# Two transformer blocks on one core: part-wise waits in the first experts' loop over further blocks, row stores without landing waits, and one exponential per head in the scan chunks

## The chip, the cores and the metric

The kernel runs on one core of a Trainium2 chip. The metric is device time in microseconds (us) of one execution. The kernel before took 2706.3 us (median of 3 runs, 2701.29 to 2710.79). The engines are TensorE (PE; its weight loads are listed as PEld), VectorE (DVE), ScalarE (ACT), GpSimd (POOL) and SyncE (SP, which issues most DMAs). A name with a q (SPq, PEq) is that engine's sequencer.

## What is computed

Two blocks in a row on 512 tokens of width 1024. The first mixes latent attention and a retention, then 32 routed experts (4 per token). The second mixes a bidirectional Mamba-2 scan with grouped attention, then 16 routed experts. Three places matter here: the modulation rows, one expert block, and the part of the scan inside a chunk of 128 tokens.

```
mod = (silu(c) @ w_ada + b_ada).reshape(B, 6, 1, D)        # same for c_ctx, and for the second block's w_mod

def expert_block(args):                                     # 32 rows of one expert at a time in the kernel
    tok, g, e = args
    u = (h_pad[tok] @ w1[e] + b1[e])
    glu = minimum(u[:, 0::2], 7); lin = clip(u[:, 1::2], -7, 7)
    act = glu * sigmoid(1.702 * glu) * (lin + 1.0)
    y = act @ w2[e] + b2[e]

# scan, one direction (the other runs on flipped inputs with its own dt and A), per chunk:
xdt = xs * dt[..., None]
a_cs = cumsum(dt * A)
decay = where(lower, exp(where(lower, a_cs[q] - a_cs[s], 0)), 0)
cb = einsum('bcqgn,bcsgn->bcqsg', Cc, Bc)
y_diag = einsum('bcqsgr,bcsgrp->bcqgrp', cb[..., None] * decay, xdt)
```

## The kernel before, in words

The program is a sequence of stages. `stage` opens a block with one instruction stream per engine; the next stage begins when all five streams have come to their end, so a wait at the end of SP's stream holds every engine. Inside a stage the streams are ordered by semaphores alone.

**Modulations.** `Modulations` spreads six groups of work g over stages of the first mixer. A group is four weight pieces of 2 MB (`load`, `load_after`), their products on PE (`product`), a bias product, a copy of the sum from PSUM to `kept[g % 2]` on ACT (`keep`), a turn into columns on PE (`turn`) and a copy of these on ACT (`keep_columns`). Some chunks are also stored as rows in DRAM (`store_rows`): groups 1 and 2 store two rows of 512 numbers, groups 4 and 5 four, groups 0 and 3 none. Group 1 is stored at the end of the stage "ret_prep" (just before the retention's loop), group 2 at the end of "ret_out" (just before the stage "latents"), groups 4 and 5 at the end of the head norms.

**First experts.** `first_expert_blocks` has 80 blocks of 32 rows laid out ahead, 31 turns of six weight chunks each (UC = 4 of `w_mlp1`, WC = 2 of `w_mlp2`, 2 MB a chunk, a ring of 11 slots). Then comes a loop over further blocks, whose number the router decides (`over_count`, never less than one). One pass of the loop loads six chunks and a bias of 8 KB, gathers and turns the rows, runs the first product on the four chunks of `w_mlp1`, the activation on DVE and ACT, and the second product on the two chunks of `w_mlp2`. The trace has 192 chunk loads, 31 x 6 + 6, so the loop runs once. Before the change the seven loads of a pass share one semaphore, and both PE and DVE wait for all of it:

```
pe.wait_ge(s.over_landed, i * (16 * LOADS) + 16 * LOADS)      # LOADS = per + 1 = 7
```

**Chunks of the scan.** `within_chunks` (stage "within") walks over eight pairs m: four token tiles t by two groups g, eight heads (r) in a pair. The exponents of both directions are formed against rows in `weight_slots`, which `load_scan` brings from DRAM, 2 MB for a tile. Per pair, DVE lowers the forward exponents below zero (`lower`, eight instructions), ACT cuts the backward ones (eight Relu), ACT takes two exponentials, DVE multiplies both by the masked product `cb`, and PE multiplies the two matrices of each head with `xdt`, which POOL made from `xs` and `dt`. `keep` masks `cb` twice and `add` adds PE's sum to the output, both on DVE.

## Time and profile before

| | us |
|---|---|
| median of 3 runs | 2706.3 (2701.29 to 2710.79) |
| the profiled execution | 2707.46 |
| its span, first to last instruction | 2705.7 |
| PE busy | 2176.6 (80%) |
| DVE busy | 1049.1 (39%) |
| ACT busy | 728.7 (27%) |
| POOL busy | 256.1 (9%) |

The trace is of one execution. Its times are counted from the span's start. Busy shares are means over stages that have different limits; three short stretches matter here: about 190 to 203 and 267 to 298 us (row stores), 1596 to 1652 us (the loop over further blocks) and 2229 to 2302 us (the scan chunks). A line of the timeline may merge several instructions of one kind; its second column is then from the start of the first to the end of the last. "Idle before" is the time in which the engine had nothing to run, and the name behind the arrow is what ended it.

### The profile page before, as it was taken

The page shows a single profiled execution, that of the slowest core. Times are in us where ns is not written, and L with a number is a line of the kernel's source. Part 1 is how long each engine was busy: PE and PEld are TensorE (multiplying, and loading weights), DVE is VectorE, ACT ScalarE, POOL GpSimd, SP SyncE. Part 2 cuts the span into 40 slices and gives each one's busy share as a digit, 9 for nine tenths or more (in the row PEclk, how much of TensorE's full clock was granted, in tenths as well). Part 3 has the DMA queues.
Part 4 walks back from the last instruction along what each step waited for, and adds up shares of the span by engine and source line. Part 5 has one row for each costly group of instructions (what it writes and reads, how often), then busy time and mean ns, then how long its engine had stood idle before and what let it go on. Part 6 is the DMA issues. An engine that isn't in the chain of part 4 may idle for free. (4 is left out here: it accounts for less than half of the span.)

```text
span 2705.7 us, 43890 instructions
## 1 busy us (share of the span) xinstructions
PE 2176.6 (80%) x18172; PEld 1252.9 (46%) x18172; DVE 1049.1 (39%) x1937; ACT 728.7 (27%) x1816; POOL 256.1 (9%) x223
## 2 busy tenths in 40 slices
PE   4979679839998998988989874799899768393795
PEld 2965247633333333333333331588766528382342
DVE  2235465442222222222222223454266567625343
ACT  3213456221110110110110100352266644412222
POOL 0001000000000000000000002000199131000001
PEclk8988879959999999998998986899999885696897
DMA  5345620138999999999999994322000011201995
GB/s 216 110 187 198 264 103 1 70 131 338 421 421 420 417 421 423 420 421 421 421 421 421 421 405 165 121 93 78 1 1 1 1 63 63 109 32 49 391 419 214
DMA packets 146299, 628.56 MB, mean 232 GB/s; under 512 B 33396, under 2 KB 64372, under 8 KB 92344
## 3 DMA queue, kind: packets, MB, share of 16 engines
q1 hardware_dynamic: 117832, 580.28, 52.9%
q0 software_dynamic: 8064, 29.36, 2.8%
q10 hardware_dynamic: 20208, 16.15, 1.8%
q8 instruction: 143, 2.34, 0.4%
q14 instruction: 52, 0.43, 0.0%
HBM read 592.37 MB, written 33.38 MB: 231 GB/s over the span
## 5 line engine op out<-in xcount | busy, mean ns | idle before, releaser
L2121 PE MATMUL psum<-w,x 128*32 128x512 f32 x5184 | 621.4, 627 | 127.5 <-DMA w<-in_w_mlp 105.5
L2121 PEld LDWEIGHTS psum<-w,x 128*32 128x32 f32 x5184 | 164.1, 113 | 526.0 <-issue 354.0
L2277 DVE TENSOR_TENSOR u<-psum,x 128x512 f32<-128x512 f32 x81 | 56.0, 691 | 707.2 <-PE psum L2121 707.2
L731 PE MATMUL psum<-high 128*128 128x512 f32 (+3 forms) x832 | 293.5, 353 | 38.7 <-DVE low L753 37.5
L2130 PE MATMUL psum<-w,act_turned 128*32 128x256 f32 x5184 | 297.3, 382 | 3.8 <-DVE act_turned L2286 3.5
L731 PE MATMUL psum<-low,high 128*128 128x512 f32 (+3 forms) x832 | 293.1, 352 | 0.0
L731 PE MATMUL psum<-high,low 128*128 128x512 f32 (+3 forms) x832 | 292.5, 352 | 0.0
L2130 PEld LDWEIGHTS psum<-w,act_turned 128*32 128x32 f32 x5184 | 168.4, 111 | 160.5 <-issue 62.4
L753 DVE TENSOR_TENSOR low<-weight_slots,high 128x1024 fp32r<-128x1024 f32 (+3 forms) x84 | 89.2, 1066 | 264.8 <-ACT high L747 264.2
L731 PEld LDWEIGHTS psum<-high 128*128 128x128 f32 x832 | 159.7, 192 | 61.1 <-ACT high L747 39.5
L731 PEld LDWEIGHTS psum<-low,high 128*128 128x128 f32 x832 | 160.0, 192 | 21.0
L2218 ACT ACTIVATE sig<-glu 128x256 f32<-128x256 f32 x81 | 34.5, 426 | 500.5 <-DVE glu L2278 500.3
L731 PEld LDWEIGHTS psum<-high,low 128*128 128x128 f32 x832 | 159.4, 192 | 21.3
L747 ACT CAST high<-weight_slots 128x1024 fp32r<-128x1024 f32 (+3 forms) x84 | 77.0, 921 | 295.2 <-PE psum L731 287.4
L2209 ACT ACTIVATE x<-psum,cols,scale1f 128x128 f32<-128x128 f32 x160 | 58.2, 470 | 205.4 <-PE psum L2121 170.5
L1203 ACT ACTIVATE weight_slots<-psum,shifts 128x768 f32<-128x768 f32 x96 | 86.7, 903 | 66.5 <-DVE shifts L1255 66.3
L2092 POOL DMA_INDIRECT x<-token_rows,slot_token x20 | 19.0, 948 | 903.3 <-PE psum L2112 879.6
L344 PE MATMUL psum<-weight_slots,mix 128*32 128x512 f32 x384 | 58.9, 755 | 56.2 <-DMA weight_slots<-in_w_ada 32.0
L1254 DVE TENSOR_REDUCE peaks<-psum 128x1 f32<-128x768 f32 x96 | 91.5, 953 | 26.9 <-PE psum L1123 26.4
L2226 ACT COPY x<-psum 128x256 f32<-128x256 f32 x80 | 29.8, 373 | 242.2 <-DMA slot_rows<-x 152.9
L2432 PE MATMUL psum<-gu,turned 128*32 128x512 f32 x656 | 82.6, 623 | 13.1 <-ACT turned L2565 5.4
L1134 PE MATMUL psum<-ident,weight_slots 128*128 128x128 f32 x576 | 85.3, 278 | 3.7 <-ACT weight_slots L1203 3.2
(497 smaller groups left out, 2846.8 us busy)
## 6 DMA issues: line engine op xcount, KB each, us to landing
w<-in_w_mlp SPq DMA_DIRECT2D x192, 2048.0 KB, 28.8
weight_slots<-in_w_ada SPq DMA_DIRECT2D x12, 2048.0 KB, 10.8
weight_slots<-in_w_mod SPq DMA_DIRECT2D x12, 2048.0 KB, 10.9
weight_slots<-in_w_in SPq DMA_DIRECT2D x9, 2048.0 KB, 8.8
gu<-in_w_gate SPq DMA_DIRECT2D x16, 1024.0 KB, 28.5
gu<-in_w_up SPq DMA_DIRECT2D x16, 1024.0 KB, 30.5
down<-in_w_down SPq DMA_DIRECT2D x16, 1024.0 KB, 31.9
weight_slots<-in_w_out SPq DMA_DIRECT2D x6, 2048.0 KB, 11.3
```

The lines of the kernel that those rows point to most:

```text
L344: mm = pe.matmul(out[c * 32:(c + 1) * 32], self.c[:, which, kp * self.KP + i, :], rows[:, i, c * BANK:(c + 1) * BANK], start=kp == 0 and i ...
L731: mm = pe.matmul(psum[:, p.group % 8, 0:p.width], *p.operands(x, weights[:, n % 2], u * QK_ + kc, kc), start=p.first and u == 0 and kc == ...
L747: act.copy(w.high[:, n % 2, :, 0:chunks[j].source.shape[2]], piece(j, u)).then_inc(s.high_made, 1)
L753: dve.tensor_tensor(w.low[at], piece(j, u), w.high[at].bitcast(F32), ALU.subtract).then_inc(s.low_made, 1)
L1134: mm = pe.transpose(turned_ps[j % 2][:, t * P:(t + 1) * P], probs[head % 2][:, t, j * P:(j + 1) * P], k.ident[:])
L1203: act.activation(probs[c][:, t], rows_ps[t % 2], ACT.Exp, scale=scale, bias=b.shifts[:, c, t:t + 1], accum_out=b.sums[:, c, t:t + 1]).then ...
L1254: step(dve.tensor_reduce(b.peaks[:, c, t:t + 1], rows_ps[t % 2], AX, ALU.max))
L2121: mm = pe.matmul(psum[g * RB:(g + 1) * RB, bank, :], b.turned[:, kc, q * RB:(q + 1) * RB], w[:, i, g * BANK:(g + 1) * BANK], start=kc == 0 ...
L2130: mm = pe.matmul(psum[g * RB:(g + 1) * RB, 2 + parity, 0:YW], b.act_turned[:, parity, kc, :], w[:, i, g * YW:(g + 1) * YW], start=kc == 0, ...
L2209: ins = act.activation(b.turned[:, m, :], psum[:, 4 + m // 4, (m % 4) * P:(m % 4 + 1) * P], ACT.Identity, scale=k.scale1f[:, m:m + 1], bia ...
L2277: step.reach(dve.tensor_tensor(b.u[:], psum[:, bank, :], b.bias[:], ALU.add), s.biased, at + 1)
L2432: mm = pe.matmul(psum[g * RB:(g + 1) * RB, bank, :].rearrange("p (a n) -> p a n", a=2), b.turned[:, half, kc, q * RB:(q + 1) * RB], b.gu[: ...
```

## The change

There are three edits. `store_rows` no longer waits for its rows to land, except for the last group; the next store waits for the earlier ones, and the `keep` that writes a buffer again waits for the stores that read it. In the loop over further blocks the bias is requested ahead of the six chunks and has a semaphore of its own; the chunks share three semaphores by twos, and PE waits for the first pair, the second pair, and ahead of the second product the third. In the scan chunks the smaller of the forward and backward exponents is taken, one exponential is made of it, the factors `dt` of both directions go into a weight matrix with `cb`, and PE multiplies one matrix per head with `xs` itself; POOL has no work there any more.

```diff
--- before.py
+++ after.py
@@ -288,6 +288,7 @@
...
         self.landed, self.rows_stored = {}, 0
+        self.stored_by = {}
     def chunks_kept_as_rows(self, g):
...
@@ -329,10 +330,14 @@
...
         sync.wait_ge(self.k.mod_kept, g + 1)
+        if self.rows_stored:
+            sync.wait_ge(self.k.mod_stored, self.rows_stored)
         for c, lo in self.chunks_kept_as_rows(g):
...
             self.rows_stored += 16
-        sync.wait_ge(self.k.mod_stored, self.rows_stored)
+        self.stored_by[g] = self.rows_stored
+        if g == len(self.work) - 1:
+            sync.wait_ge(self.k.mod_stored, self.rows_stored)
     def product(self, pe, j):
@@ -365,6 +370,9 @@
...
             act.wait_ge(self.k.mod_turned, g - 1)
+            if self.stored_by.get(g - 2):
+                act.wait_ge(self.k.mod_stored, self.stored_by[g - 2])
         act.copy(self.kept[g % 2], self.core.psum[:, self.SUM_BANK[g], :]).then_inc(self.k.mod_kept, 1)
...
@@ -2004,7 +2012,6 @@
...
     RING = 11
-    LOADS = per + 1
     BC = BANK // RB
...
@@ -2028,9 +2035,12 @@
...
                   "clipped", "squashed", "act_ready", "y_kept", "x_turned", "x_kept", "y_stored", "vector_step",
-                  pool_dma=("gathered", "slots_free", "over_landed", "ids_made", "taken")) as (block, s):
+                  pool_dma=("gathered", "slots_free", "over_bias_landed", "over0_landed", "over1_landed", "over2_landed",
+                            "ids_made", "taken")) as (block, s):
         landed = [[s.landed0_0, s.landed0_1, s.landed0_2, s.landed0_3, s.landed0_4, s.landed0_5],
                   [s.landed1_0, s.landed1_1, s.landed1_2, s.landed1_3, s.landed1_4, s.landed1_5]]
+        over_landed = [s.over0_landed, s.over1_landed, s.over2_landed]
         def wait_landed(engine, turn, c):
@@ -2069,17 +2079,16 @@
...
                 e = sync.value_load(r.blocks[0:1, ds(i, 1)], min_val=0, max_val=E1 - 1)
+                sync.wait_ge(s.bias_spread, i + turns)
+                sync.sem_inc(s.taken, 1)
+                sync.dma_start(b.bias_in_over[:], bias_of(e)).then_inc(s.over_bias_landed, 16)
                 for c in range(per):
...
                     sync.dma_start(b.w[:, (turns * per + c) % RING].rearrange("p (k n) -> p k n", k=src.shape[1]), src)\
-                        .then_inc(s.over_landed, 16)
-                sync.wait_ge(s.bias_spread, i + turns)
-                sync.sem_inc(s.taken, 1)
-                sync.dma_start(b.bias_in_over[:], bias_of(e)).then_inc(s.over_landed, 16)
+                        .then_inc(over_landed[c // 2], 16)
         @block.gpsimd
...
@@ -2185,15 +2194,19 @@
...
                 pe.wait_ge(s.x_kept, i + (tiles + 1))
-                pe.wait_ge(s.over_landed, i * (16 * LOADS) + 16 * LOADS)
                 pe.wait_ge(s.biased, i + n)
...
                 for c in range(UC):
+                    if c % 2 == 0:
+                        pe.wait_ge(over_landed[c // 2], i * 32 + 32)
+                        pe.sem_inc(s.taken, 1)
                     first_chunk(turns, c, 0, 0).then_inc(s.slots_free, 1)
...
                 pe.wait_ge(s.y_kept, i + n)
+                pe.sem_inc(s.taken, 1)
+                pe.wait_ge(s.over2_landed, i * 32 + 32)
                 pe.sem_inc(s.taken, 1)
...
@@ -2302,7 +2315,7 @@
...
                 step.restart()
-                dve.wait_ge(s.over_landed, i * (16 * LOADS) + 16 * LOADS)
+                dve.wait_ge(s.over_bias_landed, i * 16 + 16)
                 dve.sem_inc(s.taken, 1)
...
@@ -3179,30 +3192,27 @@
...
+    n = len(pairs)
...
+    with buffers(core, decay=[P, HELD, SR * P], back=[P, 2, SR * P], weight=[P, 2, SR * P], cb=[P, 2, 2, P]) as b, \
+            stage(core, "within", "cb_summed", "cb_kept", "backward", "tinted", "lowered", "weighted", "exped", "joined",
+                  "summed", "added") as (block, s):
+        def row(t, d, g, r):
+            c = d * SH + g * SR + r
+            return core.ring.slots[:, t % 2].rearrange("p k n -> p (k n)")[:, c * P:(c + 1) * P]
+        def column(v, t, d, g, r):
+            c = d * SH + g * SR + r
+            return v[:, t, c:c + 1]
         @block.sync
         def _(sync):
...
+                sync.wait_ge(s.backward, SG * (t - 1))
...
         @block.tensor
         def _(pe):
@@ -3213,43 +3223,69 @@
...
+                pe.wait_ge(s.joined, m + 1)
...
+                    mm = pe.matmul(psum[:, 4 + m % 2, r * SP_:(r + 1) * SP_], b.decay[:, m % HELD, r * P:(r + 1) * P],
+                                   xs[:, t, (g * SR + r) * SP_:(g * SR + r + 1) * SP_], start=True, stop=True)
...
         @block.scalar
         def _(act):
...
+            def backward(m):
+                t, g = pairs[m]
...
+                if m >= 2:
+                    act.wait_ge(s.lowered, m - 1)
...
+                    ins = act.activation(b.back[:, m % 2, r * P:(r + 1) * P], row(t, 1, g, r), ACT.Identity,
+                                         bias=column(w.fallen, t, 1, g, r))
+                ins.then_inc(s.backward, 1)
+            def tint(m):
+                t, g = pairs[m]
+                act.wait_ge(s.cb_kept, 2 * m + 2)
+                if m >= 2:
+                    act.wait_ge(s.joined, m - 1)
+                for r in range(SR):
+                    ins = act.activation(b.weight[:, m % 2, r * P:(r + 1) * P], b.cb[:, m % 2, 1], ACT.Copy,
+                                         scale=column(w.dt, t, 1, g, r))
+                ins.then_inc(s.tinted, 1)
+            def exponential(m):
...
+                act.activation(b.decay[:, m % HELD], b.decay[:, m % HELD], ACT.Exp).then_inc(s.exped, 1)
+            backward(0)
+            tint(0)
+            exponential(0)
+            backward(1)
+            tint(1)
+            for m in range(n):
+                if m + 1 < n:
+                    exponential(m + 1)
+                if m + 2 < n:
+                    backward(m + 2)
+                    tint(m + 2)
         @block.vector
         def _(dve):
+            def keep(m):
+                if m % 4 == 0:
+                    dve.wait_ge(s.cb_summed, m // 4 + 1)
+                if m >= 2:
+                    dve.wait_ge(s.tinted, m - 1)
+                    dve.wait_ge(s.weighted, m - 1)
+                for d in range(2):
+                    dve.tensor_tensor(b.cb[:, m % 2, d], psum[:, 6 + m // 4, (m % 4) * P:(m % 4 + 1) * P],
+                                      k.after[:] if d else k.upto[:], ALU.mult).then_inc(s.cb_kept, 1)
             def lower(m):
...
@@ -3257,23 +3293,24 @@
...
+                dve.wait_ge(s.backward, m + 1)
...
+                    at = slice(r * P, (r + 1) * P)
+                    ins = dve.scalar_tensor_tensor(out=b.decay[:, m % HELD, at], in0=row(t, 0, g, r),
+                                                   scalar=column(w.fallen, t, 0, g, r), in1=b.back[:, m % 2, at],
+                                                   op0=ALU.add, op1=ALU.min)
...
+            def weigh(m):
+                t, g = pairs[m]
+                dve.wait_ge(s.tinted, m + 1)
+                dve.wait_ge(s.cb_kept, 2 * m + 2)
+                for r in range(SR):
+                    at = slice(r * P, (r + 1) * P)
+                    ins = dve.scalar_tensor_tensor(out=b.weight[:, m % 2, at], in0=b.cb[:, m % 2, 0],
+                                                   scalar=column(w.dt, t, 0, g, r), in1=b.weight[:, m % 2, at],
+                                                   op0=ALU.mult, op1=ALU.add)
+                ins.then_inc(s.weighted, 1)
             def add(m):
...
@@ -3281,24 +3318,24 @@
...
+            keep(0)
+            keep(1)
...
+            weigh(0)
+            for m in range(n):
+                if m + 1 < n:
...
+                dve.wait_ge(s.exped, m + 1)
+                dve.wait_ge(s.weighted, m + 1)
+                dve.tensor_tensor(b.decay[:, m % HELD], b.decay[:, m % HELD], b.weight[:, m % 2], ALU.mult)\
+                    .then_inc(s.joined, 1)
+                if m + 1 < n:
+                    weigh(m + 1)
...
+                if m + 2 < n:
+                    keep(m + 2)
+            add(n - 1)
...
```

SP's issues in one pass of the loop over further blocks, before (`w` are the chunks, `x<-in_b_mlp` is the bias; each ISA row is a semaphore step):

```order
L2077 DMA w<-in_w_mlp 128x4096
L2074 REGISTER_ALU
L2077 ISA
L2077 DMA w<-in_w_mlp 128x4096
L2080 REGISTER_ALU
L2082 ISA
L2082 DMA x<-in_b_mlp 128x16
```

And now, from the same pass:

```order
L2084 ISA
L2084 DMA x<-in_b_mlp 128x16
L2087 ISA
L2090 ISA
L2090 DMA w<-in_w_mlp 128x2x2048
L2087 REGISTER_ALU
L2090 ISA
L2090 DMA w<-in_w_mlp 128x2x2048
```

The bias moved from behind the sixth chunk to ahead of the first.

ACT in the scan chunks, the first pairs, before (L3242 is the Relu on the backward exponents, L3246 and L3248 are the exponentials):

```order
L3242 ACTIVATE decay<-weight_slots,running 128x128 x8
L3246 ACTIVATE decay<-decay 128x1024
L3248 ACTIVATE decay<-decay 128x1024
L3242 ACTIVATE decay<-weight_slots,running 128x128 x8
L3246 ACTIVATE decay<-decay 128x1024
```

And now (L3245 is `backward`, L3256 `tint`, L3262 the one exponential):

```order
L3245 ACTIVATE back<-weight_slots,fallen 128x128 x8
L3256 ACTIVATE weight<-cb,dt 128x128 x8
L3262 ACTIVATE decay<-decay 128x1024
L3245 ACTIVATE back<-weight_slots,fallen 128x128 x8
L3256 ACTIVATE weight<-cb,dt 128x128 x8
L3262 ACTIVATE decay<-decay 128x1024
```

One exponential of a pair went, eight narrow activations came.

DVE in the scan chunks, one pair in the middle, before (L3262 `lower`, L3295 the multiplications by `cb`, L3274 `keep`, L3282 `add`):

```order
L3282 TENSOR_TENSOR raw<-raw,psum 128x512
L3262 SCALAR_TENSOR_TENSOR decay<-weight_slots,fallen,zero 128x128 x8
L3295 SCALAR_TENSOR_TENSOR decay<-decay,cb 128x1024 x2
L3274 TENSOR_TENSOR cb<-psum,upto 128x128
L3274 TENSOR_TENSOR cb<-psum,after 128x128
```

And now (L3299 `lower`, L3330 the one multiplication, L3310 `weigh`, L3319 `add`, L3286 `keep`):

```order
L3299 SCALAR_TENSOR_TENSOR decay<-weight_slots,fallen,back 128x128 x8
L3330 TENSOR_TENSOR decay<-decay,weight 128x1024
L3310 SCALAR_TENSOR_TENSOR weight<-cb,dt,weight 128x128 x8
L3319 TENSOR_TENSOR raw<-raw,psum 128x512
L3286 TENSOR_TENSOR cb<-psum,upto 128x128
L3286 TENSOR_TENSOR cb<-psum,after 128x128
```

One wide multiplication of a pair went, eight narrow instructions of `weigh` came, and `keep` moved to the pair's end, two pairs ahead.

## Rows read from the trace of the kernel before

**Rows 1.** Timeline, end of "ret_prep": start us, length us, engine, line, what [idle before].

```profile
192.66 0.56 SPq L333 DMA_DIRECT2D rows<-mix  x2
...
194.60 0.19 ACT L374 COPY cols<-psum 128x32 f32<-128x32 f32 x1 [1.96 <-PE psum L358]
202.59 1.28 ACT L1399 ACT_TABLE_LOAD   x1 [7.80 <-PEq L168]
```

**Rows 2.** Timeline, from the end of the retention to the end of "latents".

```profile
267.89 1.91 ACT L1533 ACTIVATE squares<-mix 128x2048 f32<-128x2048 f32 x1 [0.44 <-ACT mix L1411]
...
274.45 0.38 SPq L308 DMA_DIRECT2D weight_slots<-in_w_mod  x1
...
275.14 0.56 SPq L333 DMA_DIRECT2D rows<-mix  x2
...
279.61 2.29 DVE L1551 TENSOR_TENSOR mix<-mix,gate 128x2048 f32<-128x2048 f32 x1
...
287.88 4.97 PE L344 MATMUL psum<-weight_slots,mix 128*32 128x512 f32 x32 [6.97 <-PEq L168]
...
295.64 0.19 ACT L374 COPY cols<-psum 128x32 f32<-128x32 f32 x1 [1.15 <-PE psum L358]
296.24 0.61 DVE L857 TENSOR_SCALAR pc<-pc,rates 128x128 f32<-128x128 f32 x2
```

**Rows 3.** DMA view, the load issued at 274.45: size, us from issue to landing.

```profile
weight_slots<-in_w_mod SPq DMA_DIRECT2D x1, 2048.0 KB, 13.1
```

**Rows 4.** Timeline, the loop over further blocks.

```profile
1602.56 0.34 SPq L2077 DMA_DIRECT2D w<-in_w_mlp  x1
1603.23 0.33 SPq L2082 DMA_DIRECT2D x<-in_b_mlp  x1
...
1615.68 2.26 ACT L2249 ACTIVATE x<-psum,cols,scale1f 128x32 f32 x8 [3.31 <-issue]
...
1631.65 8.94 PE L2121 MATMUL psum<-w,x 128*32 128x512 f32 x64 [18.69 <-DMA x<-in_b_mlp]
...
1643.29 0.63 DVE L2286 STREAM_TRANSPOSE act_turned<-act 128x256 f32<-128x256 f32 x1 [0.24 <-DVE act L2283]
...
1644.07 3.66 PE L2130 MATMUL psum<-w,act_turned 128*32 128x256 f32 x64 [3.47 <-DVE act_turned L2286]
```

**Rows 5.** DMA view, the two issues at 1602.56 and 1603.23.

```profile
w<-in_w_mlp SPq DMA_DIRECT2D x1, 2048.0 KB, 23.3
...
x<-in_b_mlp SPq DMA_DIRECT2D x1, 8.0 KB, 28.2
```

**Rows 6.** Stage view of "within": us, busy PE, PEld, DVE, ACT, POOL, PEclk, DMA, GB/s.

```profile
2229.00:2301.00 72.00, 59.11 (x272) 58.33 (x272) 55.40 (x105) 34.96 (x80) 15.23 (x8) 0.52 0.15 59
```

**Rows 7.** Groups by line, same stage: count | busy us, mean ns | idle before.

```profile
L3223 PE MATMUL psum<-xdt,decay 128*128 128x64 f32 x256 | 55.4, 422 | 12.1 <-DVE decay L3295 12.1
...
L3282 DVE TENSOR_TENSOR raw<-raw,psum 128x512 f32<-128x512 f32 x8 | 5.5, 683 | 16.2 <-PE psum L3223 16.2
```

**Rows 8.** Timeline, the scan chunks.

```profile
2229.26 7.62 POOL L3202 TENSOR_TENSOR xdt<-xs,dt 128x1024 f32<-128x1024 f32 x4 [21.62 <-POOLq L168]
...
2229.54 8.54 DVE L3262 SCALAR_TENSOR_TENSOR decay<-weight_slots,fallen,zero 128x128 f32<-128x128 f32 x8
...
2238.40 2.17 DVE L3262 SCALAR_TENSOR_TENSOR decay<-weight_slots,fallen,zero 128x128 f32<-128x128 f32 x8
...
2240.50 2.35 DVE L3295 SCALAR_TENSOR_TENSOR decay<-decay,cb 128x1024 f32<-128x1024 f32 x2
...
2243.16 2.17 DVE L3262 SCALAR_TENSOR_TENSOR decay<-weight_slots,fallen,zero 128x128 f32<-128x128 f32 x8
...
2244.25 2.43 ACT L3242 ACTIVATE decay<-weight_slots,running 128x128 f32<-128x128 f32 x8
...
2246.59 1.04 ACT L3246 ACTIVATE decay<-decay 128x1024 f32<-128x1024 f32 x1
...
2301.59 1.28 ACT L3319 ACT_TABLE_LOAD   x1 [16.74 <-PEq L168]
```

61 lines of the change are left out of this document (removed).

## The prediction

> **What bounds the kernel now.** I read the slices first: PE is busy 80% of the span, but the edits do not touch the long matmul stretches. So I read the timeline of each stage that the diff names, looking for what ends the last wait there.
>
> At the end of "ret_prep" SP issues two small row stores at 192.66 and the last engine, ACT, ends at 194.79; nothing runs until ACT starts at 202.59 [rows 1]. The reader is to see a stage held open by the landing of 4 KB. "ret_out" repeats it: stores at 275.14, DVE ends at 281.90, the next stage opens at about 287.87 [rows 2]. The stores sit behind 2 MB weight pieces; the one issued at 274.45 needs 13.1 us and lands at 287.55 [rows 3].
>
> In the loop over further blocks PE starts at 1631.65, ended by the bias, though the rows it multiplies were ready at 1615.68 + 2.26 = 1617.94 [rows 4]. The sixth chunk, issued at 1602.56, lands 23.3 us later at 1625.9, the bias, issued last at 1603.23, at 1631.4 [rows 5]. In the scan chunks PE is busy 59.11 of 72 us with DVE close behind at 55.40, at a granted clock of 0.52, so 1.2 GHz nearly throughout [rows 6]. PE's 256 matmul records there take 55.4 us, 0.216 each [rows 7]. DVE loses time to something besides: the first eight `lower` take 8.54 us while POOL runs four multiplications, the second eight 2.17 without POOL [rows 8].
>
> **Part A, the row stores.** A stage opens 0.44 us after the last engine's end (ACT at 267.89) [rows 2]. "ret_prep" without SP's wait ends with ACT at 194.79, so the retention starts at 195.23 instead of 202.59: −7.4. What is late next there? The retention's own modulation products read pieces requested well before, and its first work needs no DMA, so I charge nothing; if it waited for the piece still in flight, which is what held the stage, the loss would be all 7.4.
>
> "ret_out" ends at 281.90, so "latents" opens 5.5 us earlier, at 282.34. But PE's second half of the products there needs the piece that lands at 287.55 [rows 3]. The 32 records took 4.97 us, so half of them 2.5 by the mean, 0.6 less or 0.8 more by the clock they get (estimates around that mean). PE's products end at 289.4 to 290.8 instead of 292.85. From there to the column copy's end is 295.83 − 292.85 = 3.0 us, some 1.7 more if its two PE groups run at the low clock: 292.4 to 295.5. DVE's end moves to 296.85 − 5.5 = 291.3. The stage ended at 296.85; it now ends by PE's chain, between 1.4 and 4.5 earlier; I take the middle, −3.0. In the head norms the final wait stays and the edit moves nothing: 0. The added waits on ACT are for stores long landed: 0. A = −10.4, bounds −3 and −12.
>
> The Trainium skill (DMA: Bandwidth & Descriptors, section on the anatomy of one DMA) gives a small DMA a fixed cost of about 2.0 us. An estimate by that page would let the stores land at about 195.2, 0.4 us behind ACT's end, and part A would be worth 0.4 us at its first place. The trace has the stage closed 9 us after the issue, so I go by the row: the price is the queue ahead, not the DMA itself.
>
> **Part B, the loop.** Bytes and issuing engine are unchanged. Moving the bias ahead makes SP wait for DVE's last static bias spread before it requests the chunks; but 23.3 us from issue to landing shows a queue deep enough to cover a request that is late by a few us, so it does not run dry and the sixth chunk's landing stays: 1625.9 by its row, at the worst 1631.4, when the old bias landed behind it. The bias now lands before any chunk of the pass, DVE spreads it early. PE starts when ACT has the rows, 1617.94 instead of 1631.65. From PE's start to the second product's start is 1644.07 − 1631.65 = 12.42 us (8.94 of it matmuls partly at the low clock, then DVE and ACT) [rows 4]. That gives 1617.94 + 12.42 = 1630.4. The third pair of chunks lands between 1625.9 and 1631.4, so the second product starts between 1630.4 and 1631.4; I take 1630.9: 1644.07 − 1630.9 = −13.2. What follows (3.66 us of matmuls, copy, store) moves along. B = −13.2, bounds −13.7 and −9.
>
> The lower bound is the clock. Before, PE idled 3.47 us ahead of the second product and still ran it in 3.66 us, at 2.4 GHz. The Trainium skill (TensorE: Matmul & The Clock Gate, Part 1) says that the throttled 1.2 GHz is the default and only activity releases it. By that rule a slightly longer idle here, or a first product broken by a chunk wait, leaves the second at 1.2 GHz; from the row that is 3.66 us more, and B is −9.5.
>
> **Part C, the chunks.** Prices from rows 8: eight narrow DVE instructions 2.10 us (2238.40 to 2240.50); two wide multiplications and two of `keep` 2.66 (2240.50 to 2243.16), the two wide 2.26 (2.35 less the overlap of the last), so 1.13 for one and 0.40 for `keep`; eight narrow activations 2.34 (2244.25 to 2246.59); the exponential 1.04; `add` 0.69 [rows 7]; PE for a pair 16 records instead of 32, 16 x 0.216 = 3.46.
>
> DVE per pair: lower 2.10, multiply 1.13, weigh 2.10, add 0.69, keep 0.40, sum 6.42. ACT per pair: 2.34 + 2.34 + 1.04 = 5.72. PE 3.46. So DVE is the bound and ACT fits under it, if `tint` (a Copy with a scale from SBUF, absent before) costs what the Relu costs. Chain at the opening, on ACT from 2229.25: backward 0, tint 0, exponential 0, backward 1 = 2.34 + 2.34 + 1.04 + 2.34 = 8.1, to 2237.3; then on DVE lower 1 and multiply 0, 3.2, to 2240.5. From there to multiply 1 it is 6.42 less the missing add, 5.7; five full periods, 32.1; the last, without lower and keep, 3.9: 2282.2. PE's last pair 3.5, the last add 0.7, hand-overs of 0.1 each about 0.4: 2286.8. The stage ended 0.44 ahead of 2301.59, at 2301.15 [rows 8]. C = −14.4.
>
> The cover: POOL's multiplications vanish, and with them the 8.54 − 2.17 = 6.4 us that DVE lost at the opening. Rows loaded for tiles 2 and 3 are requested about as early as before. Bounds: the nearest rows for `tint` are the Relu's 2.34 and 2.26 for eight narrow reads of PSUM [rows 4]; should it cost half as much again, 3.5 for eight, ACT needs 6.9 a pair and with its hand-overs about 7.1, 0.7 more than DVE's 6.42, eight times: with it C = −9; and if the clock rises, PE's last pair shortens by 1.7: C = −16. The next stage has no PE work for 30 us in either kernel, so its clock is not touched.
>
> **Sum.** Profiled execution 2707.5 − 10.4 − 13.2 − 14.4 = 2669.5. The median of the runs lies 1.2 below the profiled time, so I forecast 2669 us, 1.4% faster.
>
> **The rivals.**
> 1. Landings take back A: the pieces still in flight decide the retention's start as well as "latents", so A is only the 3 us at its low bound. For: the stores behind those pieces had not landed until about 202 [rows 1]. Against: the first products there read earlier pieces. 2707.5 − 3 − 13.2 − 14.4 − 1.2 = 2676.
> 2. ACT becomes the bound of the chunks, or the hand-overs between ACT and DVE cost more: C = −9, with the second product of the loop at 1.2 GHz (B = −9.5): 2707.5 − 10.4 − 9.5 − 9 − 1.2 = 2677.
> 3. The DMA side of the loop is late: SP's wait ahead of all chunks lets the queue run dry and every landing slips by some 5 us (the distance between the last two landings, 1631.4 − 1625.9). B = −8: 2674.
> 4. Slower than before: ACT and DVE take turns in the chunks, since each of `tint`, `weigh`, `lower` and the exponential waits for the other engine's last group. Fully in turn a pair costs 6.42 + 5.72 = 12.1 us, eight 97, with opening and tail 103 against 72: +31. With A and B at −21 (their forecasts less 3) that is 2707.5 − 21 + 31 − 1.2 = 2716. It decides from a period of 11.9 us a pair on, where C eats A and B. Against it: in the written order each group on one engine has about 3 us of other work beside it (`keep` for pair m+2 stands ahead of lower and multiply, 3.2 us, while `tint` needs 2.34).
>
> **Chances.** Forecast 0.67, rival 1 0.10, rival 2 0.10, rival 3 0.08, rival 4 0.02, something unseen that leaves it unchanged 0.03. A measurement here can tell about 0.3%, 8 us. The forecast and the first three rivals are all over 30 us faster: faster 0.95, same 0.03, slower 0.02. Range: best ends of all three (−12, −13.7, −16) give 2665, and the three runs of before spread by 5 us to either side, so 2660 below; rivals 1 to 3 reach 2677, with spread 2682 above.
>
> **What would show it.** The gap ahead of the retention's first ACT row falls from 7.80 to about 0.4 us. "latents" opens about 7 us after its stores' issue instead of 12.7, and its PE row splits around a DMA wait. PE's first row in the loop follows ACT's L2249 group directly; DVE's wait for the bias is gone; the second product waits for activation or the third pair by at most 1 us. "within" lasts about 57.5 us, DVE busy about 90% of it, its first eight `lower` near 2.2 us, PE at 1.2 GHz with 128 records. The forecast is wrong if "within" takes over 64 us, if the retention starts with a DMA wait, or if the second product starts later than 14 us after the first.

## The result, and the profile after

| | before | changed |
|---|---|---|
| median of 3 runs, us | 2706.3 (2701.29 to 2710.79) | 2670.4 (2663.18 to 2673.84) |
| profiled execution, us | 2707.46 | 2663.18 |
| its span, us | 2705.7 | 2661.0 |
| mean granted clock of PE | 0.882 | 0.889 |

The ratio is 0.9861 (95% interval 0.9827 to 0.9895), so the change saves 1.4%. The forecast was 2669 us, range 2660 to 2682. The changed kernel was run five more times later: 2670.71 us (2667.85 to 2680.52), ratio 0.9866 (0.9846 to 0.9886). Note that the profiled execution is the lowest of its three runs, 7.2 us below the median; what it shows beyond the median has to be explained apart.

The page of the changed kernel, its first lines (engine, busy us, share, instructions):

```profile
span 2661.0 us, 43762 instructions
...
PE 2150.0 (81%) x18044; PEld 1224.9 (46%) x18044; DVE 1044.6 (39%) x1992; ACT 740.0 (28%) x1872; POOL 241.7 (9%) x215
```

PE has 128 instructions fewer, the matmuls of the chunks. POOL is busy 14.4 us less and ACT 11.3 us more, which is the chunks too. The rest of the change does not show on the page; the places have to be read one by one.

**Part A, first place.** Timeline of the changed kernel at the end of "ret_prep" (start, length, engine, line, what, idle before), to hold against [rows 1]:

```profile
192.29 0.56 SPq L336 DMA_DIRECT2D rows<-mix  x2
...
194.23 0.19 ACT L382 COPY cols<-psum 128x32 f32<-128x32 f32 x1 [1.97 <-PE psum L363]
194.75 1.28 ACT L1407 ACT_TABLE_LOAD   x1 [0.33 <-PEq L168]
```

ACT's gap ahead of the retention was 7.80 us and is 0.33. The retention opens 7.84 us earlier, at 194.75. What the stores waited behind before the change shows in the DMA view: the last weight piece ahead of them, issued at 190.16 (size, us from issue to landing),

```profile
weight_slots<-in_w_ada SPq DMA_DIRECT2D x1, 2048.0 KB, 12.0
```

landed at 202.2, and the stage closed 0.4 us later, at 202.59. In "ret_out" the piece landed at 287.55 and the stage closed at 287.87.

**Part A, second place.** PE in the changed kernel, from the stores' stage into the stage behind "latents", to hold against [rows 2]:

```profile
264.94 1.92 PE L349 MATMUL psum<-weight_slots,mix 128*32 128x512 f32 x16 [1.34 <-DMA weight_slots<-in_w_mod]
269.92 3.61 PE L349 MATMUL psum<-weight_slots,mix 128*32 128x512 f32 x16 [3.06 <-DMA weight_slots<-in_w_mod]
275.35 1.92 PE L349 MATMUL psum<-weight_slots,mix 128*32 128x512 f32 x16 [1.81 <-DMA weight_slots<-in_w_mod]
277.20 1.06 PE L355 MATMUL psum<-mix,ones 1*32 1x512 f32 x8
278.97 1.06 PE L363 MATMUL psum<-pick,mix 128*128 128x8 f32 x8 [0.70 <-ACT mix L376]
280.61 2.79 PE L503 MATMUL psum<-ident,px 128*128 128x128 f32 x12 [0.58 <-PEq L168]
```

The row at 275.35 is the last product of the group: it is now broken off from the one before and ended by a DMA. The stage opened earlier and met the weight piece that is still in flight, as forecast.

**Part B.** The loop over further blocks in the changed kernel, to hold against [rows 4]:

```profile
1598.66 2.27 ACT L2262 ACTIVATE x<-psum,cols,scale1f 128x32 f32 x8 [3.12 <-issue]
1601.42 8.61 PE L2130 MATMUL psum<-w,x 128*32 128x512 f32 x64 [5.28 <-ACT x L2262]
...
1612.72 0.63 DVE L2299 STREAM_TRANSPOSE act_turned<-act 128x256 f32<-128x256 f32 x1 [0.24 <-DVE act L2296]
1614.44 5.35 PE L2139 MATMUL psum<-w,act_turned 128*32 128x256 f32 x64 [4.41 <-DMA w<-in_w_mlp]
```

PE's 18.69 us of waiting for a DMA became 5.28 us ended by ACT's rows. The second product is ended by the third pair of chunks, 1.1 us after DVE's turn is done (1612.72 + 0.63 = 1613.35); and it takes 5.35 us where it took 3.66. DMA view of the changed kernel, the sixth chunk, issued at 1585.73, to hold against [rows 5]:

```profile
w<-in_w_mlp SPq DMA_DIRECT2D x1, 2048.0 KB, 28.6
```

It lands at 1614.33, and PE is let go 0.1 us later, at 1614.44.

**Part C.** Groups by line in the chunks of the changed kernel (count | busy us, mean ns | idle before), then one pair on the timeline. [Rows 6 to 8] are their counterparts.

```profile
L3231 PE MATMUL psum<-xs,decay 128*128 128x64 f32 x128 | 29.4, 424 | 23.7 <-DVE decay L3330 23.7
...
L3256 ACT ACTIVATE weight<-cb,dt 128x128 f32<-128x128 f32 x64 | 19.5, 387 | 3.4 <-DVE cb L3286 3.4
...
L3310 DVE SCALAR_TENSOR_TENSOR weight<-cb,dt,weight 128x128 f32<-128x128 f32 x64 | 17.5, 355 | 0.0
L3299 DVE SCALAR_TENSOR_TENSOR decay<-weight_slots,fallen,back 128x128 f32<-128x128 f32 x64 | 17.5, 353 | 1.2 <-ACT back L3245 1.2
L3330 DVE TENSOR_TENSOR decay<-decay,weight 128x1024 f32<-128x1024 f32 x8 | 9.8, 1229 | 0.0
```

```profile
2198.36 2.48 ACT L3245 ACTIVATE back<-weight_slots,fallen 128x128 f32<-128x128 f32 x8 [1.63 <-PEq L168]
...
2209.02 1.22 DVE L3330 TENSOR_TENSOR decay<-decay,weight 128x1024 f32<-128x1024 f32 x1
...
2210.15 2.19 DVE L3310 SCALAR_TENSOR_TENSOR weight<-cb,dt,weight 128x128 f32<-128x128 f32 x8
...
2212.65 2.18 DVE L3299 SCALAR_TENSOR_TENSOR decay<-weight_slots,fallen,back 128x128 f32<-128x128 f32 x8
...
2214.75 1.22 DVE L3330 TENSOR_TENSOR decay<-decay,weight 128x1024 f32<-128x1024 f32 x1
```

DVE's rows hardly wait (the 0.0 and 1.2 in the last column), so DVE is the bound; PE, at 29.4 us, waits 23.7 us for it. From the first ACT row to the next stage's first ACT row (2256.26) the stage takes 57.90 us; it took 2301.59 − 2229.25 = 72.34.

### The profile page after: what moved, and what is told of

It is laid out like the page before. It is cut to its first block and busy times, and to the rows that moved or that the text cites. A ratio compares the mean times of both kernels' runs of the same rounds, so it can differ in the third digit from the quotient of the medians.

```text
span 2661.0 us, 43762 instructions
## 1 busy us (share of the span) xinstructions
PE 2150.0 (81%) x18044; PEld 1224.9 (46%) x18044; DVE 1044.6 (39%) x1992; ACT 740.0 (28%) x1872; POOL 241.7 (9%) x215
## 5 line engine op out<-in xcount | busy, mean ns | idle before, releaser
L2139 PE MATMUL psum<-w,act_turned 128*32 128x256 f32 x5184 | 302.8, 387 | 4.7 <-DMA w<-in_w_mlp 4.4
L349 PE MATMUL psum<-weight_slots,mix 128*32 128x512 f32 x384 | 57.8, 740 | 55.4 <-DMA weight_slots<-in_w_ada 31.7
## 6 DMA issues: line engine op xcount, KB each, us to landing
gu<-in_w_gate SPq DMA_DIRECT2D x16, 1024.0 KB, 28.9
```

What stands on the lines that cost most here:

```text
L349: mm = pe.matmul(out[c * 32:(c + 1) * 32], self.c[:, which, kp * self.KP + i, :], rows[:, i, c * BANK:(c + 1) * BANK], start=kp == 0 and i ...
L2139: mm = pe.matmul(psum[g * RB:(g + 1) * RB, 2 + parity, 0:YW], b.act_turned[:, parity, kc, :], w[:, i, g * YW:(g + 1) * YW], start=kc == 0, ...
```

## The experiments

Ratios are to the kernel before, run on the same chip beside the others: 2704.02 us beside a_only, b_only, c_only and bias_first, 2706.32 us beside land1, whole, pool_busy and twice, 2709.21 us beside the rest. A gain in us behind a ratio is the ratio's distance from one, times that. The table holds stage lengths read off ACT's timeline in each profile: the gap ahead of the retention, the retention, "ret_out", "latents", the loop from ACT's rows to the next stage, and the chunks.

| kernel | median us | gap | retention | ret_out | latents | loop | chunks |
|---|---|---|---|---|---|---|---|
| before | 2706.3 | 7.80 | 65.30 | 19.98 | 10.67 | 37.48 | 72.34 |
| changed | 2670.4 | 0.33 | 60.51 | 14.56 | 11.91 | 26.36 | 57.90 |
| changed, again | 2670.7 | 0.33 | 60.52 | 14.55 | 14.40 | 26.62 | 57.92 |
| a_only | 2691.6 | 0.33 | 62.13 | 14.56 | 15.57 | 37.67 | 72.34 |
| b_only | 2696.6 | 7.77 | 65.28 | 19.62 | 10.26 | 28.58 | 72.34 |
| c_only | 2695.9 | 9.12 | 60.49 | 19.87 | 11.08 | 43.08 | 57.91 |
| land1 | 2680.5 | 9.21 | 60.51 | 14.56 | 11.65 | 26.48 | 57.90 |
| whole | 2683.6 | 0.33 | 60.51 | 14.56 | 14.57 | 37.58 | 57.91 |
| bias_last | 2675.0 | 0.33 | 60.51 | 14.56 | 12.12 | 31.15 | 57.92 |
| pool_busy | 2680.5 | 0.33 | 60.51 | 14.56 | 14.25 | 26.34 | 68.51 |
| twice | 2684.5 | 0.33 | 60.50 | 14.56 | 14.27 | 26.64 | 67.88 |
| bias_first | 2670.8 | 0.33 | 62.14 | 14.56 | 15.65 | 28.50 | 57.90 |
| early10 | 2667.7 | 0.33 | 62.47 | 14.56 | 10.84 | 26.94 | 57.92 |

Read it by columns: gap, "ret_out" and chunks repeat within 0.1 us wherever nothing was done to them in the changed kernel, while the retention (60.5, 62.1 or 65.3) and "latents" (11.7 to 15.7) differ between profiles of the same code. These two get their own paragraph below.

### Each part by itself

a_only is the kernel before with the edits of `store_rows` and `keep`:

```diff
-        sync.wait_ge(self.k.mod_stored, self.rows_stored)
+        self.stored_by[g] = self.rows_stored
+        if g == len(self.work) - 1:
+            sync.wait_ge(self.k.mod_stored, self.rows_stored)
```

> Only the row stores' edit. Theory of separate stage waits: the retention opens 7.8 us earlier and the stage behind latents 4.2 us earlier again, 12.0 us in all, 2694 us. Rival, the clock: the retention's further 4.8 us in the changed kernel's profile comes from the shorter idle stretch ahead of it and belongs to the edit: 16.8 us, 2689.5. If it is chance of one execution, the retention lasts 65 us from its first ACT row in some profiles and 60.5 in others, whatever the kernel. Rival, nothing: the landings are waited for elsewhere, within 2 us of the kernel before.

Measured: 2691.6 us (2690.29 to 2693.52), ratio 0.9951 (0.9934 to 0.9967), 13 us faster (9 to 18).

b_only has the edits of the loop over further blocks:

```diff
-                pe.wait_ge(s.over_landed, i * (16 * LOADS) + 16 * LOADS)
...
+                        pe.wait_ge(over_landed[c // 2], i * 32 + 32)
...
-                dve.wait_ge(s.over_landed, i * (16 * LOADS) + 16 * LOADS)
+                dve.wait_ge(s.over_bias_landed, i * 16 + 16)
```

> Only the loop over further blocks. Theory: PE starts its first product when ACT has the rows and its second when the third pair of chunks lands, 11 to 13 us less, 2694 to 2695 us; with the second product partly at 1.2 GHz 11. Rival, the gain is given back where the next stage starts on bandwidth or stores: under 5 us.

Measured: 2696.64 us (2689.88 to 2702.07), ratio 0.9966 (0.9953 to 0.998), 9 us faster (5 to 13).

c_only has the new scan chunks:

```diff
-    with ... "within", "xdt_made", ...
+    with ... "within", "cb_summed", "cb_kept", "backward", "tinted", "lowered", "weighted", "exped", "joined",
...
+            def tint(m):
...
+            def weigh(m):
```

> Only the scan chunks. Theory, DVE is the bound at 6.3 us a pair: the stage lasts 57.6 us instead of 72.0, 14.4 us less, 2692 us. Rival, part of that was the other edits' shift: under 10 us.

Measured: 2695.89 us (2684.4 to 2700.91), ratio 0.9964 (0.9947 to 0.9981), 10 us faster (5 to 14).

The three sum to 32 us; the whole change has 37.6 us by its own ratio and 36.3 by the later one, within what three intervals of 4 us to either side leave. So the parts add up as far as can be told; an interplay of a few us is not excluded. The medians are too coarse to tell 9 from 14 us; c_only's stage is 14.43 us shorter in its profile, while the loop of the same profile, whose code is the one of before, is 5.6 us longer (PE is let go 1.8 us later, and its two products take 3.5 us more at the lower clock).

a_only's 9 to 18 us holds both its theory (12.0) and its rival (16.8, with the shorter retention counted to the edit), so it does not decide between them.

### Was the landing of the stores the gap?

land1 puts the wait back for group 1 alone:

```diff
-        if g == len(self.work) - 1:
+        if g == 1 or g == len(self.work) - 1:
```

> The changed kernel, with the landing wait back for group 1 alone. Theory: the stage ahead of the retention stays open for 7.8 us more, 2678 us. Rival, the clock: if the idle stretch ahead of the retention costs it TensorE clock as well, 12.6 us more, 2683, and the retention lasts about 65 us from its first ACT row, not 60.5.

Measured: 2680.53 us (2670.3 to 2685.22), ratio 0.9911 (0.9893 to 0.9929). The gap is back, timeline of this kernel:

```profile
189.18 0.37 SPq L309 DMA_DIRECT2D weight_slots<-in_w_ada  x1
...
190.78 0.56 SPq L336 DMA_DIRECT2D rows<-mix  x2
...
191.90 0.19 ACT L382 COPY cols<-psum 128x32 f32<-128x32 f32 x1 [1.15 <-PE psum L363]
201.29 1.28 ACT L1407 ACT_TABLE_LOAD   x1 [9.21 <-PEq L168]
```

From the stores' issue to the opening it is 201.29 − 190.78 = 10.5 us (9.9 before), although PE's turn was 0.8 us shorter here and ACT done earlier. So the gap follows the landing of the stores and not the work: a faster PE only waits longer. The gap itself is worth 7.5 to 8.9 us, by how early ACT is done. The retention took 60.51 us here, not the 65 of the rival. But this profile, at 2670.30 us, is the lowest of four runs; the others took 2677.88 to 2685.22. By the ratios the wait costs 12 to 13 us, with some 7 us to either side, which holds the theory's 7.8 and the rival's 12.6. That the gap is the landing is shown; whether it costs the retention clock as well in other executions is not.

### What of part B is the bias, what the waits by pairs?

whole keeps the bias ahead and lets PE wait for all six chunks:

```diff
-                    if c % 2 == 0:
-                        pe.wait_ge(over_landed[c // 2], i * 32 + 32)
-                        pe.sem_inc(s.taken, 1)
+                    if c == 0:
+                        for part in over_landed:
+                            pe.wait_ge(part, i * 32 + 32)
+                            pe.sem_inc(s.taken, 1)
```

> The changed kernel, but PE waits for all six chunks ahead of the first product; the bias stays ahead of them. It shows what the bias's place alone is worth. Theory: PE starts when the sixth chunk lands, about 17.6 us behind its turning of the rows less what the transfer row says, so between 14 us (a landing at 1625.9 on the first kernel's clock) and 19.8 us (1631.6) after that turn's start at its 0.; the second product 12.4 behind. The parts' waits are worth 8 to 13 us: 2678 to 2683. If the bias had been the whole cost before, the time would stay at 2670 to 2672.

Measured: 2683.57 us (2680.36 to 2686.73), ratio 0.9914 (0.9897 to 0.9931). PE on the timeline of this kernel (its ACT rows begin at 1604.58):

```profile
1620.38 8.96 PE L2130 MATMUL psum<-w,x 128*32 128x512 f32 x64 [18.32 <-DMA w<-in_w_mlp]
...
1632.96 3.66 PE L2139 MATMUL psum<-w,act_turned 128*32 128x256 f32 x64 [3.62 <-DVE act_turned L2300]
```

bias_last does the opposite, the bias back behind the chunks with a semaphore of its own:

```diff
-                sync.wait_ge(s.bias_spread, i + turns)
-                sync.sem_inc(s.taken, 1)
-                sync.dma_start(b.bias_in_over[:], bias_of(e)).then_inc(s.over_bias_landed, 16)
                 for c in range(per):
...
+                sync.wait_ge(s.bias_spread, i + turns)
+                sync.sem_inc(s.taken, 1)
+                sync.dma_start(b.bias_in_over[:], bias_of(e)).then_inc(s.over_bias_landed, 16)
```

> The changed kernel, with the bias request put back behind the six chunks of the loop over further blocks (with its own semaphore), PE's waits by pairs of chunks kept. The bias then lands with or behind the last chunk, and only then does DVE spread it (1.05 us) and start the activation (about 3.2 us), so the second product starts 4 to 5 us later: 2674 to 2675. Rivals: the place of the bias is worth nothing (2670), or it carries the whole of part B, as the wait's name before suggested (2681).

Measured: 2674.95 us (2667.22 to 2680.96), ratio 0.9882 (0.9865 to 0.9899). DVE and PE on the timeline of this kernel (its ACT rows begin at 1595.82):

```profile
1598.57 8.73 PE L2131 MATMUL psum<-w,x 128*32 128x512 f32 x64 [5.30 <-ACT x L2263]
...
1611.56 1.03 DVE L2287 STREAM_TRANSPOSE x<-x 128x512 f32<-128x512 f32 x1 [23.20 <-DMA x<-in_b_mlp]
...
1615.35 0.63 DVE L2300 STREAM_TRANSPOSE act_turned<-act 128x256 f32<-128x256 f32 x1 [0.24 <-DVE act L2297]
1616.28 4.98 PE L2140 MATMUL psum<-w,act_turned 128*32 128x256 f32 x64 [8.99 <-DVE act_turned L2300]
```

Count each from the start of ACT's rows. In the kernel before, PE was released at 1631.65 − 1615.68 = 15.97 us; in whole at 1620.38 − 1604.58 = 15.80; in the changed kernel the third pair released it at 1614.44 − 1598.66 = 15.78; in bias_last the bias released DVE at 1611.56 − 1595.82 = 15.74. The last chunk and the bias land together: in bias_last the DMA view has them at 1611.1 and 1611.4. Hence moving the bias alone, which is whole, is worth nothing in the loop (37.58 us against 37.48), though the name that ended PE's wait before was the bias. The waits by pairs with the bias behind bring 37.48 − 31.15 = 6.3 us, and the bias ahead another 4.5 to 4.8: DVE's spread and the activation then lie before the last landing. The bias's place has its worth only once the wait is split; together the two edits have 11. These are readings of single profiles; the medians of whole (2683.6) and bias_last (2675.0) against 2670.5 order the same way.

### What of part C is POOL, and does more work on PE raise its clock?

pool_busy gives POOL its eight multiplications back, their result unused:

```diff
+        @block.gpsimd
+        def _(pool):
+            for t in range(TX):
...
+                for d in range(2):
+                    pool.tensor_tensor(b.xdt[:, t % 2, d].rearrange("p (h e) -> p h e", e=SP_),
```

> The changed kernel with POOL's eight multiplications back in the scan chunks; their result is not used. Theory, POOL and DVE exclude each other while both read two operands from SBUF: the groups of eight narrow DVE instructions beside a POOL pair take 4.7 us and more instead of 2.2, and the stage, bound by DVE, grows by the 10 to 15 us of POOL's work: 2680 to 2685. Rival, only the opening suffers as POOL has slack later: 6 us more at most. Rival, no contention: the same time.

Measured: 2680.51 us (2679.77 to 2683.98), ratio 0.9908 (0.9891 to 0.9924); the stage 10.6 us longer. POOL and DVE on the timeline of this kernel:

```profile
2206.18 7.64 POOL L3207 TENSOR_TENSOR xdt<-xs,dt 128x1024 f32<-128x1024 f32 x4 [21.59 <-POOLq L168]
...
2209.08 6.20 DVE L3311 SCALAR_TENSOR_TENSOR decay<-weight_slots,fallen,back 128x128 f32<-128x128 f32 x8
2215.20 2.18 DVE L3322 SCALAR_TENSOR_TENSOR weight<-cb,dt,weight 128x128 f32<-128x128 f32 x8
```

Eight `lower` take 6.20 us beside POOL and 2.18 without, and the groups of `lower` and `weigh` rise from 17.5 and 17.5 us to 21.5 and 24.0: 10.5 us, all of the stage's difference. With DVE the bound, all that POOL takes from DVE is on the path.

twice makes each head's product twice and adds it, so the scan's inner output is doubled:

```diff
-                    mm = pe.matmul(psum[:, 4 + m % 2, r * SP_:(r + 1) * SP_], ..., start=True, stop=True)
+                    for d in range(2):
+                        mm = pe.matmul(psum[:, 4 + m % 2, r * SP_:(r + 1) * SP_], ..., start=d == 0, stop=d == 1)
```

> The changed kernel with each head's product made twice into the same sum (the scan's inner output is doubled), so PE has its 256 records back. Theory, DVE at 6.33 us a pair was the bound and PE would need 6.9 at 1.2 GHz: the period becomes 6.9 to 7.2 us, with the last pair's 3.5 more the stage grows by 7 to 10 us: 2678 to 2680. Rival, the clock rises to 2.4 GHz with the denser work: PE needs 3.5 a pair and the stage grows by under 2 us.

Measured: 2684.51 us (2681.63 to 2686.26), ratio 0.9918 (0.9901 to 0.9934). The stage took 67.88 us. Its groups by line, and the stage in one row (us, busy PE, PEld, DVE, ACT, POOL, granted clock, DMA):

```profile
L3232 PE MATMUL psum<-xs,decay 128*128 128x64 f32 x256 | 54.9, 421 | 8.1 <-DVE decay L3331 8.1
```

```profile
2206.00:2273.00 67.00, 58.45 (x272) 58.18 (x272) 50.77 (x160) 46.00 (x136) 0.00 (x0) 0.53 0.16 64
```

PE busy 58 of 67 us does not lift the clock from 1.2 GHz (0.53), and 256 products cost 54.9 us as they did before (55.4). So the halved count of products is needed too: with all of them PE would be the bound, 10 us later. The two causes of part C overlap; each put back alone takes some 10 of its 14.4 us.

### Can what is left be had?

bias_first moves the 128 KB bias of the stage behind the loop ahead of its four pieces of x:

```diff
+            if bias is not None:
+                sync.dma_start(b.bias[:], bias).then_inc(s.bias_loaded, 16)
...
-            if bias is not None:
-                sync.dma_start(b.bias[:], bias).then_inc(s.bias_loaded, 16)
```

> The changed kernel, and in the combining stage behind the first experts the 128 KB bias is requested ahead of the four 512 KB pieces of x instead of behind them. In the changed kernel PE waited 10.4 us there for the bias. Theory, the same mistake as in the loop (a small load queued behind bulk that is needed later): PE starts about 8 us earlier and the stage ends 4 to 8 us earlier, 2663 to 2666 us. Rival, the stage is held by POOL's gathers or by the x pieces, which are late instead: within 2 us of 2670.

Measured: 2670.8 us (2666.58 to 2672.07), ratio 0.9871 (0.9852 to 0.989): no gain. PE's first row there in the changed kernel and then in this one; then DVE in this one:

```profile
1635.41 13.99 PE L2704 MATMUL psum<-bias,spread_turned 32*128 32x512 f32 x16 [10.42 <-DMA bias<-in_b_mlp]
```

```profile
1634.15 13.99 PE L2704 MATMUL psum<-bias,spread_turned 32*128 32x512 f32 x16 [1.61 <-DMA bias<-in_b_mlp]
```

```profile
1645.67 1.28 DVE L2722 SCALAR_TENSOR_TENSOR total<-got,gates,psum 128x1024 f32<-128x1024 f32 x1 [25.57 <-DMA gate<-rows]
```

PE's wait fell from 10.42 to 1.61 us, and DVE, whose first row there was released by PE before, now waits for the gate, the last of the same queue: the stage takes 50.39 us against 50.69. It is the trap of part B over again, one wait taken away ahead of another that ends at nearly the same time.

early10 makes one product of part A's second place in the retention, so that a weight slot comes free sooner:

```diff
@@ the retention's stage, SyncE @@
                 mod.load_after(sync, 12)
+                mod.load_after(sync, 13)
@@ the retention's stage, TensorE, behind products 8 and 9 @@
+                mod.product(pe, 10)
@@ ret_out @@
-            mod.load_after(sync, 13)
...
-            mod.product(pe, 10)
```

> The changed kernel, with the modulations' product 10 made in the retention stage right behind products 8 and 9 and the load of piece 13 issued there, ahead of the stage "ret_out". If the 4 us that part A gives back in "latents" are PE's wait for the last weight piece, an earlier free slot lets that piece be requested about 5 us earlier: "latents" falls from 11.9 (or 14.3 to 15.7) us to 10.5 or less, the retention grows by at most 1 us, and the time is 2666 to 2669. Rival: the retention is bound by PE and takes back the 1.9 us of the product and more, or the pieces are bound by the queue and not by their request: within 1 us of the changed kernel.

after_again is the changed kernel itself, run beside early10 and bias_last.

> The changed kernel once more, unchanged. My reading that the profiled execution's extra 7 us over the parts' sum are the clock that it happened to get expects a median of 2670 (2 to either side), and a retention that lasts 60.5 us or 62 to 65 with no edit between. If the extra gain belongs to the change, the profiled execution lies at 2663 again with 60.5 and 11.9 us in the two stages.

Measured: early10 2667.68 us (2666.61 to 2670.31), ratio 0.9851 (0.9836 to 0.9866); after_again 2670.71, ratio 0.9866. PE in "latents" of early10, to hold against the row at 275.35 above:

```profile
269.58 5.85 PE L349 MATMUL psum<-weight_slots,mix 128*32 128x512 f32 x32 [3.18 <-PEq L168]
275.36 1.06 PE L355 MATMUL psum<-mix,ones 1*32 1x512 f32 x8
```

The two products are one row again and no DMA ends a wait: the piece is there when the stage opens. "latents" took 10.84 us and not 14.40. The retention took 62.47 against 60.52, which looks like the 1.9 us of the product that was put into it, as the rival says. Row by row it is not. A part of the product fills a gap in which PE otherwise idles 1.1 to 1.2 us: the first row behind it (L1454) starts 10.63 us into the stage, and the same row in the changed kernel 10.29 us, so it costs 0.34 us. The other 1.6 us arise at the end of the stage, in products that the edit does not touch. The first of them in the changed kernel, in early10 and in a_only:

```profile
248.57 1.16 PE L1463 MATMUL psum<-px,weights 128*128 128x128 f32 x8 [0.78 <-DVE weights L1502]
```

```profile
246.69 2.02 PE L1464 MATMUL psum<-px,weights 128*128 128x128 f32 x8 [0.78 <-DVE weights L1504]
```

```profile
243.79 1.66 PE L1463 MATMUL psum<-px,weights 128*128 128x128 f32 x8 [0.78 <-DVE weights L1502]
```

In the ten microseconds with these rows the granted clock is 1.00 in the changed kernel and 0.83 in the other two. a_only and bias_first have the same 1.6 us without the moved product. So the edit itself kept to the expected 1 us in the retention. Over the four stages early10 has 88.20 us, after_again 89.80 and the changed kernel's first profile 87.31. The median is 3 us lower, and the intervals overlap: early10 is perhaps the better kernel, which is not shown.

### What differs between profiles of the same code

The retention took 65.30 us before and 60.51 after, which no edit asks for. Its beginning on PE, slices of the stage (us, busy PE, PEld, DVE, ACT, POOL, granted clock, DMA share, GB/s), first before, then changed:

```profile
213.00:223.00 10.00, 10.00 (x21) 4.18 (x22) 5.14 (x7) 2.32 (x3) 0.11 (x1) 0.63 0.99 376
223.00:268.00 45.00, 43.14 (x255) 30.88 (x257) 26.65 (x33) 10.81 (x16) 5.30 (x6) 0.97 0.55 194
```

```profile
205.00:215.00 10.00, 9.96 (x50) 6.09 (x51) 7.49 (x10) 3.06 (x5) 2.88 (x3) 1.00 1.00 378
215.00:255.00 40.00, 38.41 (x222) 26.16 (x220) 24.28 (x30) 10.12 (x14) 3.16 (x4) 1.00 0.63 222
```

In the second ten microseconds PE is busy with hardly a pause in both, and the clock is 0.63 in the one and 1.00 in the other. c_only has the code of before in this place and 60.49 us; land1 has 9 us of idle ahead of it and 60.51. So the old code does not always bring the 65.3, nor does the idle time. But it is not shown that the edit has no part in it: the 65.3 stands in two of the three profiles without the row stores' edit (before and b_only, with gaps of 7.80 and 7.77 us) and in none of the ten with it, and c_only and land1 were both profiled in executions 6.5 and 10 us below their medians. The 62.1 us of a_only and bias_first are another thing: the clock rises as early as in the changed kernel and falls once near the end of the stage, in the rows shown for early10. "latents" goes the same way: the last product, the bias and the turn take 1.92, 1.06 and 1.06 us in the changed kernel's first profile, and 3.64, 1.93 and 1.87 in this one, a_only:

```profile
272.45 3.64 PE L349 MATMUL psum<-weight_slots,mix 128*32 128x512 f32 x16 [3.64 <-DMA weight_slots<-in_w_mod]
276.02 1.93 PE L355 MATMUL psum<-mix,ones 1*32 1x512 f32 x8
278.65 1.87 PE L363 MATMUL psum<-pick,mix 128*128 128x8 f32 x8 [0.70 <-ACT mix L376]
```

What sets the clock's rise or its fall at one time rather than at another I cannot say from these runs.

## Why the prediction was right, step by step

| term | forecast | in the first profile | over all profiles |
|---|---|---|---|
| A, first place | −7.4 | −7.8 | −7.5 to −8.9 |
| A, second place | −3.0 (−1.4 to −4.5) | −4.2 | −0.4 to −4.4 |
| B | −13.2 (−13.7 to −9) | −11.1 | −8.9 to −11.1 |
| C | −14.4 | −14.4 | −14.4 |
| sum | −38.0 | −37.5 | |

**A, first place.** Right: nothing was late behind it. Forecast opening 195.23, measured 194.75, with PE 0.4 us earlier on its own. The row on the stores' stage, and not the bare cost of a small DMA, was the price. land1 shows that the wait is the gap; that the stores are late because of the piece ahead is read from the two places where that piece lands 0.3 to 0.4 us ahead of the opening, and no run moved the piece. The figure of about 2.0 us that the prediction took from the Trainium skill (DMA: Bandwidth & Descriptors, section on the anatomy of one DMA) is given there for DMAs issued by GpSimd; these are issued by SP, and from issue to the closing of the stage the trace has 9.9 us (the prediction says 9).

**A, second place.** Right in its mechanism and, over the profiles, somewhat too large. "ret_out" is 5.4 us shorter each time (forecast 5.5) and PE then waits for the last piece in "latents". In six of the nine profiles with this edit and the pieces unmoved, "latents" takes 14.25 to 15.65 us, where PE runs the last product, the bias or the turn at 1.2 GHz behind its waits. I had allowed 2.5 us for this beside the mean; three breaks in PE's work (1.34, 3.06 and 1.81 us in the first profile) stand ahead of it, and the low clock is the more frequent case here.

**B.** The mechanism was right: PE starts on ACT's rows and the second product on the third pair. The start was right within a microsecond: 15.78 us behind ACT's first row where I had 1630.9 − 1615.68 = 15.2. So the step brings 28.39 − 15.78 = 12.6 us. In b_only, bias_first and early10 the first product ran slower (10 us for 8.6), and the activation, not the third pair, let the second one start. The rest is rival 2's: the second product runs partly at 1.2 GHz (granted 0.69), 5.35 us for 3.66, and takes 1.7 back. It takes 4.91 to 6.58 us in all nine profiles with the waits by pairs; of the four with one wait for everything three have 3.66, c_only 6.49. So the low clock is the rule behind the split waits and the exception without them. The Trainium skill (TensorE: Matmul & The Clock Gate, Part 1) names 1.2 GHz the default; that fits, but why the split brings it is not shown: no wait breaks the first product of the changed kernel (one row of 8.61 us), and PE idles 3.62 us ahead of the second in b_only (6.58 us) and in whole (3.66 us) alike. The prediction held the low clock as a bound of 3.66 us, and the value taken should have had about half of it. One reading was wrong without harm: I took 1625.9, 23.3 us from issue in the DMA view [rows 5], for the earliest time at which the sixth chunk could be used. PE is not let go by it until 15.8 us behind ACT's rows, which is 1631.5 in the times of before, at the upper end of my interval (1631.4). The three profiles in which the seven loads share one semaphore have 23.3, 23.3 and 25.2 us for the sixth chunk; the ten in which each pair has its own have 28.2 to 28.9, and wherever an engine waited for it, it was let go 0.1 to 0.2 us after that. bias_last, whose bias comes last as before, has 28.2, so it is not the order of the issues. The view could be trusted for a load with a semaphore of its own or of its pair, and of loads on a shared one only for the last.

**C.** Right to 0.1 us, which is partly luck. From the first wide multiplication to the second it is 2214.75 − 2209.02 = 5.73 us, the 5.7 that the forecast gives a pair without `add`. The opening took 0.5 us longer than forecast, and from the first to the last wide multiplication it was 41.2 us for 41.7; the two cancel. ACT waits 3.4 us for DVE's `keep`, in pieces of 0.6 a pair at most, and follows DVE. `tint` costs what the Relu cost (2.43 for eight); the first eight `lower` take 2.18 us (forecast "near 2.2"); the clock stayed at 1.2 GHz. POOL's work was no side remark: pool_busy puts its removal at 10.6 us of the stage.

**The rivals.** Rival 1 (A only 3 us) fell with the first row of the retention. Rival 2 came true in its small half, the clock in B, and not in the chunks. Rival 3 (the queue runs dry): the third pair releases PE as late as whole's six chunks do, and as late as before, so nothing slipped against ACT's rows. Rival 4 (turns between ACT and DVE) fell: the two run side by side.

**The rest.** The prediction's own sum is 2707.46 − 38.0 − 1.2 = 2668.3, which it rounds to 2669. With the parts as measured, medians against medians, it is 2706.3 − 37.5 = 2668.8, against 2670.4. The profiled run is 44.3 us below the one of before, 6.8 more than the parts: 4.8 are the clock in the retention, which the forecast left unchanged, and the rest comes from stages that I did not take apart. The second profile of the same kernel, at the median, has 60.52 us in the retention too; its span is 7.6 us longer, 2.5 of it in "latents", 0.3 in the loop and the rest in stages outside the change. So a median within 2 us of the forecast is partly luck: the retention's 4.8 us less is made up for by losses elsewhere, and a single profile moves by some 5 us to either side.

## What to carry to other kernels

A wait for several DMAs shows one name, the last; before moving that one ahead, ask when the others have landed, and expect nothing unless the wait itself is split. The landing of a store that nobody reads soon can cost as much as what stands before it in the queue (here 12 us of a 2 MB load, for 4 KB), and should be waited for where its data or buffer is needed. When new waits stand ahead of PE's work, price a part of it at the low clock. When a stage grows by just the length of what was put into it, look at the rows behind before calling it the cause: in early10 the product cost 0.3 us and the clock the rest.

## What the runs showed of the hardware that was not expected

- The same instructions in the same order took 60.5, 62.1 or 65.3 us in one stage: 65.3 where the granted clock rose late (0.63 in the second ten microseconds, PE busy in all of them), 62.1 where it fell once near the end (0.83). 9 us of idle ahead (land1, c_only) still gave 60.5.
- PE busy 58.45 of 67 us with fp32 matmuls of 64 columns was granted 0.53, no more than with half of them (busy 33.10 of 58 us, 0.53).
- Eight narrow VectorE instructions took 6.20 to 8.54 us beside GpSimd's multiplications and 2.17 without; 19.8 us of GpSimd work that nobody waits for cost the stage 10.6 us.
- For the sixth of seven loads on one shared semaphore the DMA view gave 23.3 to 25.2 us from issue to landing (three profiles), and 28.2 to 28.9 where pairs had their own (ten profiles), with the release 0.1 to 0.2 us behind.
